# Making the next chunk's decays and key products inside the current chunk's iteration, and masking the block inverse by predicated copies, in a hybrid recurrent decoder step

## What is computed

```python
d = jnp.cumsum(gc, axis=-1)
gam = _masked_exp(incl, d[..., :, None] - d[..., None, :])
a = jnp.where(strict, bc[..., :, None] * jnp.einsum('bhtd,bhsd->bhts', kc, kc) * gam, 0.0)
rhs = jnp.concatenate([vc * bc[..., None], kc * (bc * jnp.exp(d))[..., None]], axis=-1)
sol = lax.linalg.triangular_solve(a + eye, rhs, left_side=True, lower=True)
w_v, w_k = sol[..., :GD_DV], sol[..., GD_DV:]
u = w_v - jnp.einsum('bhld,bhde->bhle', w_k, S)
attn = jnp.einsum('bhtd,bhsd->bhts', qc, kc) * gam
o = jnp.einsum('bhtd,bhde->bhte', qc * jnp.exp(d)[..., None], S) + jnp.einsum('bhts,bhse->bhte', attn, u)
S_new = jnp.exp(dl)[..., None, None] * S + jnp.einsum(
    'bhsd,bhse->bhde', kc * jnp.exp(dl[..., None] - d)[..., None], u)
```

## Time and profile before

| | |
|---|---|
| median of three runs | 2029.15 us (2026.89 to 2031.36) |
| the profiled execution | 2037.19 us, of which the span of instructions is 2035.4 us |
| the prompt's recurrence, first layer and second layer | 200.35 us and 200.74 us |
| busy in the second layer's recurrence | PE 152.16, DVE 129.71, ACT 96.90, POOL 8.74 us |
| granted TensorE clock there | 0.91 of full speed |

### The profile page before, as it was taken

The page is one execution under the profiler, slowest core; times in us unless marked ns, Lnnn a source line. Parts: engine busy times, 40 slices in busy tenths (PEclk is TensorE's granted clock), DMA queues, the critical chain, the costliest instruction groups (busy, mean ns, idle before and its releaser), DMA issues. The chain is left out here.

```text
span 2035.4 us, 35889 instructions
## 1 busy us (share of the span) xinstructions
PE 1793.8 (88%) x13698; PEld 1709.7 (84%) x13698; DVE 935.5 (46%) x2016; ACT 818.0 (40%) x1794; POOL 96.7 (5%) x163
## 2 busy tenths in 40 slices
PE   5999967777889999999889997887688699999995
PEld 5999957765679999999789996776558699999995
DVE  4274276654543222244354634666534523224344
ACT  4235544544234333333332464455422433333333
POOL 0021010003000000000002011000200000000000
PEclk8999999986789999999989999999688899999997
DMA  5321000003372333322042210000308422323211
GB/s 169 90 83 63 1 5 1 1 1 71 103 126 83 88 88 88 103 80 72 15 137 80 69 42 4 1 1 1 67 6 145 112 86 82 93 88 110 75 39 44
DMA packets 128706, 132.82 MB, mean 65 GB/s; under 512 B 32630, under 2 KB 95522, under 8 KB 128584
## 3 DMA queue, kind: packets, MB, share of 16 engines
q1 hardware_dynamic: 128584, 131.22, 23.5%
HBM read 121.53 MB, written 9.66 MB: 64 GB/s over the span
## 5 line engine op out<-in xcount | busy, mean ns | idle before, releaser
L307 PE MATMUL bank<-arena 128*128 128x272 f32 (+4 forms) x3488 | 1015.1, 291 | 31.8 <-DVE arena L414 14.7
L309 PE MATMUL bank<-arena 128*128 128x272 f32 (+4 forms) x3488 | 1012.4, 290 | 0.0
L308 PE MATMUL bank<-arena 128*128 128x272 f32 (+4 forms) x3488 | 1008.0, 289 | 0.0
L307 PEld LDWEIGHTS bank<-arena 128*128 128x128 f32 (+1 forms) x3488 | 656.5, 188 | 38.8 <-issue 25.3
L308 PEld LDWEIGHTS bank<-arena 128*128 128x128 f32 (+1 forms) x3488 | 657.6, 189 | 3.0 <-issue 2.1
L309 PEld LDWEIGHTS bank<-arena 128*128 128x128 f32 (+1 forms) x3488 | 657.5, 188 | 0.9
L351 DVE TENSOR_TENSOR arena<-sbuf,arena 128x512 fp32r<-128x512 f32 x296 | 201.3, 689 | 346.0 <-ACT arena L347 345.9
L347 ACT CAST arena<-sbuf 128x512 fp32r<-128x512 f32 x296 | 180.7, 622 | 348.1 <-PE bank L309 303.6
L2934 DVE TENSOR_TENSOR arena<-sbuf,arena 128x544 fp32r<-128x544 f32 x88 | 63.8, 724 | 143.2 <-ACT arena L2878 143.2
L351 DVE TENSOR_TENSOR arena<-arena 128x512 fp32r<-128x512 f32 (+1 forms) x128 | 87.3, 702 | 82.6 <-ACT arena L347 82.1
L347 ACT CAST arena<-arena 128x512 fp32r<-128x512 f32 (+1 forms) x128 | 77.8, 622 | 116.1 <-PE bank L309 107.3
(11 more groups left out here) (370 smaller groups left out, 1832.2 us busy)
## 6 DMA issues: line engine op xcount, KB each, us to landing
sbuf<-in_w_gate_up SPq DMA_DIRECT2D x176, 256.0 KB, 3.1
arena<-in_w_in SPq DMA_DIRECT2D x96, 256.0 KB, 2.8
sbuf<-in_w_down SPq DMA_DIRECT2D x88, 256.0 KB, 2.6
arena<-in_w_in SPq DMA_DIRECT2D x32, 260.0 KB, 2.6
sbuf<-in_w_out SPq DMA_DIRECT2D x32, 256.0 KB, 4.4
sbuf<-in_state_gdn_S SPq DMA_DIRECT2D x8, 512.0 KB, 6.1
out_s_S<-sbuf SPq DMA_DIRECT2D x8, 512.0 KB
arena<-in_x_prompt SPq DMA_DIRECT2D x4, 512.0 KB, 7.4
```

Of the source, the lines that this page charges most:

```text
L307: pe.matmul(out, wH, hH, start=first, stop=False)
L308: pe.matmul(out, wH, hL, start=False, stop=False)
L309: return pe.matmul(out, wL, hH, start=False, stop=last)
```

## The change

- PE: `decays_and_products` becomes `decay_rows(c + 1)`, issued inside level 5 of chunk c, and `key_products(c + 1)`, issued after level 6 and `hg_scores(c, 5)`. `mix_turn(b - 1)` moves from the end of an iteration to after `inverse_start` of the following one. HGRN2's old part moves forward to levels 2 and 3. `gd_output` goes from level 2 to between levels 4 and 5.
- DVE: `decays(c + 1)` stands inside level 5 of chunk c, `inverse_start(c)` is the first thing of an iteration, ahead of `hg_place(b, 6)`, `ml_state(b - 1)`, `targets(b)` and the attention product, which was part of `inverse_start`. `A` gets two buffers.
- The maximum with 0 moves to ACT as a `Relu` (128x512).
- The mask multiplication on DVE goes. ACT copies the late columns of B0 unmasked into `p1` (`first_product`), and `update` writes the product into `X` by a predicated copy with the mask in place of the addition.
- ACT copies half of B1 to `Y` (the early columns) in place of all of it.
- HGRN2's keys and delta move from B3 to B6, half of `mix_turn` from B7 to B6.

The diff, cut:

```diff
-    edb, Dg, A, Y = t4(), t4(), t4(), t4()
+    edb, Dg, Y = t4(), t4(), t4()
+    A = two(t4)
...
-            def decays_and_products(c):
+            def decay_rows(c):
                 if c > 0:
                     pe.wait_ge(*done("bv", c - 1))
                 turn(B2, lambda h: bc(cols[:, 0, c, 4 + h:5 + h], P, P), H, "drows")
+
+            def key_products(c):
                 if c > 0:
                     pe.wait_ge(*done("X", c - 1))
                     pe.wait_ge(*done("Y", c - 1))
...
             def inverse_second(c, lv):
-                pe.wait_ge(*done("p1_masked", c, lv))
+                pe.wait_ge(*done("p1_taken", c, lv))
...
             def hg_key_turn(c):
                 pe.wait_ge(*done("hkd", c))
-                pe.wait_ge(*done("S", c))
-                turn(B3, lambda j: hkd[c % 2][:, j], 2, "hk_turned")
+                if c > 0:
+                    pe.wait_ge(*done("mix_taken", c - 1))
+                turn(B6, lambda j: hkd[c % 2][:, j], 2, "hk_turned", base=256)
...
             for i in range(CHUNKS + 1):
                 now, old = i < CHUNKS, i > 0
                 c, b = i, i - 1
                 if old:
                     kS(b)
                 if now:
-                    decays_and_products(c)
+                    hg_diagonal(c)
+                    inverse_start(c)
+                if i > 1:
+                    mix_turn(b - 1)
                 if old:
                     ml_rows(b)
...
+                    inverse_first(c, 3)
+                    value_turn(c)
+                    inverse_second(c, 3)
+                    hg_scores(c, 1)
+                if old:
+                    hg_delta(b)
+                    hg_output(b)
+                if now:
+                    inverse_first(c, 4)
+                    hg_scores(c, 2)
...
+                    inverse_second(c, 4)
                 if old:
                     gd_output(b)
                 if now:
...
+                    inverse_first(c, 5)
+                    hg_scores(c, 3)
+                    if c + 1 < CHUNKS:
+                        decay_rows(c + 1)
+                    inverse_second(c, 5)
                 if old:
                     ml_output(b)
+                    gd_delta(b)
                 if now:
...
+                    inverse_first(c, 6)
+                    hg_scores(c, 4)
+                    inverse_second(c, 6)
                 if old:
                     ml_key_turn(b)
                 if now:
...
+                    hg_scores(c, 5)
+                    if c + 1 < CHUNKS:
+                        key_products(c + 1)
...
             def decays(c):
+                act.wait_ge(*done("Dg", c))
+                if c > 1:
+                    act.wait_ge(*done("p1", c - 2))
+                a = A[c % 2]
+                act.activation(a, Dg, ACT.Relu).then_inc(sig["EAm"], 1)
                 act.wait_ge(*done("EAm", c))
-                act.activation(A, A, ACT.Exp, scale=-1.0).then_inc(sig["EA"], 1)
+                act.activation(a, a, ACT.Exp, scale=-1.0).then_inc(sig["EA"], 1)
...
-                act.copy(flat(Y), B1).then_inc(sig["Y"], 1)
+                act.copy(early(Y, lv), early(heads(B1), lv)).then_inc(sig["Y"], 1)
+
+            def first_product(c, lv):
+                act.wait_ge(*done("p1", c, lv))
+                if lv > 1:
+                    act.wait_ge(*done("p2", c, lv - 1))
+                act.copy(packed(p1, lv), late(heads(B0), lv)).then_inc(sig["p1_taken"], 1)
...
-                dve.tensor_scalar(A, Dg, 0.0, None, ALU.max).then_inc(sig["EAm"], 1)
...
-            def mask(c, lv):
-                dve.wait_ge(*done("p1", c, lv))
-                if lv > 1:
-                    dve.wait_ge(*done("p2", c, lv - 1))
-                mul(packed(p1, lv), late(heads(B0), lv), up_mask(lv)).then_inc(sig["p1_masked"], 1)
-
             def update(c, lv):
                 dve.wait_ge(*done("p2", c, lv))
                 if lv > 1:
                     dve.wait_ge(*done("turned", c, lv - 1))
-                x = late(X[c % 2], lv)
-                tt(x, x, packed(heads(B0)[:, :, 0:64], lv), ALU.add).then_inc(sig["X"], 1)
+                dve.copy_predicated(late(X[c % 2], lv), up_mask(lv).bitcast(U32),
+                                    packed(heads(B0)[:, :, 0:64], lv)).then_inc(sig["X"], 1)
```

More of the change, by code:

```diff
@@ L2691, in _ @@
                 c, b = i, i - 1
+                if now:
+                    inverse_start(c)
+                if i > 0 and i <= CHUNKS:
+                    hg_place(b, 6)
+                if i > 1:
+                    ml_state(b - 1)
                 if old:
@@ L2694, in _ @@
                 if now:
-                    decays(c)
                     hg_sums(c)
-                    inverse_start(c)
+                    attention(c)
                     hg_differences(c)
-                    mask(c, 1)
+                    update(c, 1)
                 if old:
@@ L2702, in _ @@
                 if now:
-                    update(c, 1)
-                if old:
-                    ml_differences(b)
-                if now:
-                    mask(c, 2)
                     hg_diagonal(c)
@@ L2729, in _ @@
                 if old:
[L2730 removed]
+                    ml_columns(b)
+                    hg_state(b)
                 if now:
[L2732 removed]
                     hg_place(c, 2)
@@ L2736, in _ @@
                 if old:
-                    gd_state(b)
-                    ml_keys(b)
+                    hg_gated(b)
+                if i + 1 < CHUNKS:
+                    decays(c + 1)
+                if now:
+                    hg_place(c, 3)
+                    hg_operands(c, 5)
+                if old:
                     gd_gated(b)
                 if now:
-                    mask(c, 6)
-                    hg_place(c, 3)
-                    hg_operands(c, 5)
                     update(c, 6)
                 if old:
-                    ml_state(b)
+                    ml_outputs(b)
                 if now:
@@ L2754, in _ @@
                     hg_decayed(c)
-                    hg_place(c, 6)
-                if old:
-                    hg_gated(b)
+            ml_state(CHUNKS - 1)
 def output_phase(nc, m, d, l, st):
```

163 lines of the change are left out of this document (80 added, 83 removed).

## The result

The changed kernel takes 2002.8 us (2001.12 to 2008.11, four runs) against 2030.26 us (2026.89 to 2040.46) of before beside it: ratio 0.9865, interval 0.9839 to 0.9891, 27 us less. Forecast were 36 us and 1993. The profiled execution took 2008.11 us, its instructions 2006.3, where before had 2037.19 and 2035.4.

A forecast was written before the change was run, and what follows sets the result against it. An engine-to-engine chain was taken to bound the recurrences. Levels +3.0, seams -2.8, -7.7, -7.6 and drain -6.3 gave -21.4 us per layer, about 3.4 back for clock: -18, -36 for both, 2029.15 to 1993; range 1983 to 2003 (0.66).

The forecast's parts named there:

- What bounds the stage: Two recurrences, some 200 us each: a chain going from engine to engine; its length counts, not the work.
- The seams: From a chunk's last update to the next X: 2.8, 7.7 and 7.6 us less per layer.
- The levels: From a chunk's X to its last update: together 3.0 us longer per layer, 1.5 of it in chunk 2.
- the walk: Step-by-step estimate of seams, levels and drain in the new order, from profiled durations at full clock.
- The drain: From the last chunk's last update to the recurrence's end, 35.84 us before: 6.3 us less per layer.
- The clock: PE's half-clock time in the recurrences would halve from 18%, putting about 3.4 us per layer back.
- The sum at full clock: Levels, seams and drain of one recurrence together: 21.4 us less per layer, new parts at full clock.
- the second rival: New stage as long at half clock as the old: another 3.4 us per layer back, 2000 us, chance 0.10.
- Dear copies: ACT's copies on the path cost 0.73 us each, 48 in all: 17 us more, 2010 us, chance 0.17.
- ACT as the chain in each level: Copies wait behind ACT work in every level, 2 us longer each: 63 us in all, 2056 us, chance 0.04.
- No gain as meant: Relu table loads, 20 us, 2013, no chance of its own; or another seam wait of old length, 2025, 0.03.
- Signs: Trace marks expected in chunks 1 to 3: seam, level and copy lengths, recurrences 180 to 185 us, clock over 0.91.

The follow-up runs named there:

- e1: The kernel before with only the mask part (predicated update, ACT copies), chunk order unchanged: 2036.81 us, ratio 1.0024 to before.
- e4: The changed kernel with twelve repeated transposes on PE in level 3 of chunks 1 to 3: 1989.97 us, ratio 0.9794 to before.
- e9: The changed kernel with the filler transposes of both e4 (level 3) and e5 (seams), nothing else: 1993.31 us, ratio 0.9803 to before.
- e3: The changed kernel with ml_weights behind level 3's copies on ACT and m_next behind level 3's update on DVE: 1985.88 us, ratio 0.9774 to before.
- e5: The kernel of e3 with twelve repeated transposes on PE in each seam, ahead of ml_key_turn: 1979.49 us, ratio 0.9737 to before.
- e7: The kernel of e3 with the maximum with 0 of decays moved from ACT back to DVE: 1983.25 us, ratio 0.9756 to before.

## Why the prediction was right, and where it was off

**What bounds the stage** was read right. The chain from engine to engine did set its length: moving 8 us of work off DVE alone brought nothing (`e1`), and 36 transposes more on PE per layer made it shorter (`e4`).

**The seams** (-2.8, -7.7, -7.6 forecast) came as -3.2, -7.3 and -5.9 in the changed kernel, and -3.2, -7.3 and -7.1 with the clock kept. With the clock kept `An` starts 4.95 us after the last `update`, directly behind DVE's last pieces, and the copy into `Y` takes 1.29, where I had 5.1 and 1.29. At half clock the key products end late, `An` waits 1.33 us for them and starts at 6.36 (1362.13 - 1355.77). Here is that row of DVE in `e9`, which has no idle time ahead of it:

```profile
1311.14 1.12 DVE L2531 SCALAR_TENSOR_TENSOR arena<-bank,arena 128x128 f32<-128x128 f32 x4
1312.29 1.29 DVE L2536 COPY_PREDICATED arena<-sbuf,arena 128x512 f32<-128x512 uint32 x1
```

So DVE's part of the seam was walked rightly, and the assumption of full clock did not hold. The last link was another than I had named. I had `hg_diagonal` wait for DVE's `hg_place` of level 6, until 7.9. In `e9` DVE has done it at 7.7, and PE waits on for ACT's `hg_queries` (L2290), which ends its iteration behind `outputs` and `ml_queries`, 8.2 us after the last `update`:

```profile
1314.42 1.13 PE L2002 MATMUL bank<-arena,sbuf 128*128 128x256 f32 x4 [1.74 <-ACT arena L2290]
```

That gives the 9.84 us where I had 9.4. In the changed kernel itself `hg_queries` also ends at 8.2 in the seam from chunk 1 to 2. There `An` starts at 5.83, behind key products at half clock, and the seam still takes 9.84. Only in the next one does the late `An`, with a copy of 1.48 us behind it, hold `hg_diagonal` longer than ACT does (DVE's placing ends at 9.3), and the seam takes 11.04.

**The levels.** For chunk 2 I gave 4.4, 4.9, 5.9, 5.2, 4.7 and 5.5. With the clock kept they are 4.04, 4.72, 5.89, 5.39, 4.89, 5.47: the walk was right to 0.4 us each, in sum +1.2 in this chunk against +1.5. That the single errors (from -0.4 to +0.2) nearly cancel is luck. Over the four chunks it is +3.5 against +3.0, with chunk 1 at +0.7 where I had 0.2. As the kernel ran, levels 3 and 4 took 6.58 and 6.34. `ml_weights` ahead of level 3's copies was the wait I had named, and `e3` shows it.

**The drain** (-6.3) came as -5.8, and -6.0 in `e9`. In the changed kernel `targets` starts 7.8 us after the last `update`, against 10.6 before (2.8 less, forecast 3.1). From `h` to the norms' logarithm it is 1.1 us instead of 5.8, but 1.9 more lie between `targets` and `h`: 2.8 less, forecast 3.2.

**The clock** is the term that was mis-sized. The sum at full clock was -21.4, and `e9` shows -19.5 and -19.9 in the two layers, with stretches left in the drain. I put 3.4 us per layer back, on the ground that the new stage would have half of the old one's time at half clock. It has 32.7 of 186.3 us in the second layer, by the stretches of the clock in its trace, where before had 36.9 of 200.7: 18% in both. The difference to `e9` is 8.2 and 5.4 us. So of the 6.7 and 3.5 us per layer by which the forecast of -18 was too hopeful, 4.8 and 2.0 are the clock and 1.9 and 1.5 the walk. The long idle waits of the seams are gone, but two of 1.9 us came in their place, before `p2` of level 3 and before the key turn, and I saw the first ("PE waits about 2 us in level 3"), but took a share of the old time and did not price what runs behind such a wait. Nor does such work double, as I had it: four matmuls of 1.06 us for 0.61, `p2` 1.84 for 1.16. So the second rival, that the clock stays low (2000 us, chance 0.10), is what happened, and 2002.8 us is just inside the upper end of my range (1983 to 2003). That rival should have carried more: in the trace of before a stretch at half clock begins at 1380.22, in the wait of 1.95 us that ends at 1380.51. (The clock of 1.0 for which I named is in none of them; the row of `e5` shows it.)

The Trainium skill, page "TensorE: Matmul & The Clock Gate", section "HAM oscillation — how this bites in real kernels", says that the clock falls back when PE has gaps, of an example with longer gaps than these. The runs agree, and here waits of 1.89 us were enough in part of the cases: `e4` and `e5` fill such gaps with work nobody needs, and the medians fall by 13 and 6 us.

**The other rivals.** Dear copies: no, 0.378 us. ACT as the chain in each level: only in level 3, 5.6 us a layer without the clock, and at the end of each seam with old work. No gain as meant: no.

**Signs.** Seams of 9 to 10 us (the last 11), level 3 the longest with 5.9 and copies at 0.38: seen. Recurrences of 180 to 185: missed by 1.3 and 4.1. A clock over 0.91 and `An` never waiting for the key products: missed (it waited 0.81 and 1.33 us), and seen in `e9`.

## What to carry to other kernels

When PE is one link of a chain, ask of each wait that a change leaves or makes, not only how long it is, but what PE runs behind it: here a wait of 1.9 us cost the chain up to 1.6 us more in the matmuls after it, and in one seam, where ACT was the last link, nothing. Twelve repeated transposes in a wait that is there anyway lengthened no level here, and one run with them gives an idea of how much of a stage is clock. And where an engine gets a new wait in a reordered program, look at what stands behind it: a mask that brought nothing in the old order was what the new order rested on.

## What the runs showed of the hardware

- TensorE's granted clock fell to half 0.3 to 1.7 us after the end of waits of only 1.89 us (changed kernel, second layer). With 0.57 us left of the wait in level 3 (`e4`) it did not fall there. The same wait did not always bring it down: not in level 3 of chunk 1 of the changed kernel, and not in the seams of `e4`'s second layer.
- At half clock four 128x128 matmuls took 1.06 us for 0.61. Eight 128x256 ones, 1.89 us at full clock, took 3.46 where nearly all of them lay in a half-clock stretch (`e3`, second layer, 1343.18) and 2.87 to 3.05 where the stretch ended inside them. That is 1.7 to 1.8 times, not twice the time.
- ACT's copy of 128x256 out of PSUM took 0.36 to 0.41 us, and at the lowest level, with the shortest runs, 0.37. DVE's predicated copy of the same size took 0.73 to 0.74 at the lowest level and 0.42 to 0.45 above.
- A time with no part in the change, between the two recurrences, differed by up to 14 us from one profiled execution to another (785.9 in `e7`, 799.5 in `e1`).
